# A layer's last modulation blocks, two weight splits and four row fetches moved to other places in the program

## The reference

```python
h = rms_norm(x, norm1) * (1 + sc1) + sh1
q, k, v, u = project(h, w_in)
x = x + g1 * (concat(attention(q, k, v), conv(u)) @ w_out)
h2 = rms_norm(x, norm2) * (1 + sc2) + sh2
x = x + g2 * peer(h2)          # 16384 single-neuron experts
# peer: per token 8 heads; each ranks 2 x 128 keys, takes the best 16 of the pair sums,
#       e = 16 expert numbers, g = softmax of their 16 scores; then
#       out = sum over the 128 slots of gelu(h2 . u_tab[e]) * g * v_tab[e]
```

## Time and profile before

| | us |
|---|---|
| median of 3 runs | 1755.14 (1753.58 to 1755.91) |
| the profiled execution | 1753.59 |
| its span, first to last instruction | 1751.8 |
| mean granted TensorE clock | 0.982 of full |

### The profile page before, as it was taken

How to read it: one execution, slowest core, us unless ns; L and a number is a source line. 1 busy time by engine, 2 the same in 40 slices (tenths; PEclk the granted TensorE clock), 3 DMA queues, 4 the chain that set the end, 5 groups by cost and what they waited for, 6 DMA issues and landing times.

```text
span 1751.8 us, 29907 instructions
## 1 busy us (share of the span) xinstructions
PE 1670.3 (95%) x9344; PEld 1407.0 (80%) x9344; DVE 1559.7 (89%) x3195; ACT 865.8 (49%) x2431; POOL 655.5 (37%) x644
## 2 busy tenths in 40 slices
PE   6999999999957889999999999999999999999997
PEld 4566777866636788888998989899999998999996
DVE  3887863499999989999999999999999999999998
ACT  3222574247787886444444444444444444444443
POOL 0000000034558874444444444444444444443442
PEclk9999999999977989999999999999999999999999
DMA  8343202111124878999999999999999999999996
GB/s 354 124 144 118 73 1 87 61 61 51 58 70 146 243 231 318 397 397 386 418 401 389 397 401 400 396 408 395 402 410 400 402 401 407 390 408 409 394 393 211
DMA packets 129316, 505.91 MB, mean 289 GB/s; under 512 B 9184, under 2 KB 64096, under 8 KB 79968
## 3 DMA queue, kind: packets, MB, share of 16 engines
q0 software_dynamic: 36864, 268.45, 38.0%
q1 hardware_dynamic: 92096, 236.49, 36.3%
q10 hardware_dynamic: 288, 0.13, 0.0%
HBM read 477.18 MB, written 25.10 MB: 287 GB/s over the span
## 4 chain that ended last, share of the span: by engine, by line
DVE 33%; DMA 22%; PE 21%; issue 19%; POOL 2%; ACT 1%; DVEq 1%; POOLq 0%; SPq 0%; ACTq 0%
DMA slab<-table,ixr 21%; DVE slab L1738 8%; PE psum L500 7%; DVE ulo L1629 4%; PE psum L735 3%; DVE slab L1688 3%; PE psum L823 3%; DVE slab L1728 3%; DVE vlo L1715 2%; DVE slab L1723 2%; PE psum L501 2%; PE psum L665 1%; DVE wlo L1711 1%; DVE slab L1543 1%; DVE slab L1692 1%
## 5 line engine op out<-in xcount | busy, mean ns | idle before, releaser
L1864 POOL DMA_INDIRECT slab<-table,ixr x256 | 421.5, 1647 | 608.0 <-DVE slab L1738 555.4
L844 PE MATMUL psum<-hhi,uhi 128*128 128x384 f32 x1008 | 339.2, 337 | 3.3 <-issue 3.2
L1728 DVE SCALAR_TENSOR_TENSOR slab<-slab,h2tok 128x1024 f32<-128x1024 f32 x256 | 312.3, 1220 | 29.3 <-DMA slab<-table,ixr 28.9
L844 PE MATMUL psum<-hhi,ulo 128*128 128x384 f32 x1008 | 338.1, 335 | 0.0
L844 PE MATMUL psum<-hlo,uhi 128*128 128x384 f32 x1008 | 337.6, 335 | 0.0
L1738 DVE SCALAR_TENSOR_TENSOR slab<-slab,cf 128x1024 f32<-128x1024 f32 x252 | 323.4, 1283 | 14.5
L858 PE MATMUL psum<-vhi,whi 128*128 128x512 f32 x762 | 297.2, 390 | 2.7 <-DVE wlo L1711 2.2
L858 PE MATMUL psum<-vhi,wlo 128*128 128x512 f32 x762 | 299.5, 393 | 0.0
L858 PE MATMUL psum<-vlo,whi 128*128 128x512 f32 x762 | 299.3, 393 | 0.0
L500 PE MATMUL psum<-slab 128*128 128x512 f32 x464 | 239.1, 597 | 2.1 <-ACT slab L925 1.7
L1203 ACT CAST whi<-slab 128x384 fp32r<-128x384 f32 x127 | 65.5, 515 | 305.6 <-DVE slab L1723 305.6
(11 more groups left out here) (237 smaller groups left out, 2824.2 us busy)
## 6 DMA issues: line engine op xcount, KB each, us to landing
slab<-ublk SPq DMA_DIRECT2D x64, 1024.0 KB, 9.3
slab<-vtab SPq DMA_DIRECT2D x63, 1024.0 KB
slab<-wblk SPq DMA_DIRECT2D x90, 512.0 KB, 4.6
g_dram<-slab SPq DMA_DIRECT2D x11, 1984.0 KB, 9.1
slab<-g_dram SPq DMA_DIRECT2D x31, 704.0 KB
slab<-table,ixr POOLq DMA_INDIRECT x256, 7.1
slab<-slab SPq DMA_DIRECT2D x42, 64.0 KB, 3.1
x<-x_in SPq DMA_DIRECT2D x1, 2560.0 KB, 9.7
```

Source lines behind the costliest of these rows:

```text
L844: last = pe.matmul(psum[:, b, 0:ND], w[:, c, :], m[:, c, :], start=(m_ == 0), stop=(m_ == 3 * DC - 1))
L1728: v.scalar_tensor_tensor(out=rows[:, sl % GR, 0:D], in0=rows[:, sl % GR, 0:D], scalar=1.0, in1=h2tok[:, k, :], op0=ALU.mult, op1=ALU.mult, ...
L1864: pool.indirect_dma_start(out=rows[:, sl % GR, :], out_offset=None, in_=table, in_offset=bass.IndirectOffsetOnAxis(ap=ixr[:, half, half_co ...
```

## The change

- TensorE: the last eight modulation blocks wait for `h2_tok` (the tokens copied out of banks 0 to 3) and no longer for `sk_read`; they use banks 0, 1 and 2 in place of 4, 5 and 6. The wait for `sk_read` now stands ahead of the turning of expert numbers, which uses banks 4 to 6 in place of 0 to 2.
- ScalarE: the first `u_lead` stands ahead of the last head's `weights_of`, the second right behind it, and both `copy_rows` behind that.
- GpSimd: the two first u rests are made inside the last `look_up`, ahead of its wait for `found`.
- The four row fetches of the build stand in blocks 2, 3, 4, 5, and `late_sums` and `row_numbers` behind blocks 0 and 1.
- The rest of u of step 2 is made by VectorE, at the head of `first_block`; GpSimd makes that of step 3 alone. In `first_block` the two dot products stand later.

```diff
-FETCH_AT = tuple(range(20, 20 + 16 * GR, 16))
+FETCH_AT = (2, 3, 4, 5)
...
-            pe.wait_ge(sk_read, SB)
+            pe.wait_ge(h2_tok, 2 * N_GATHER)
             for g in range(N_ADA3 // ADA_G):
-                ada(S_ADA3 + ADA_G * g, 4 + g)
+                ada(S_ADA3 + ADA_G * g, g)
             pe.wait_ge(row_copied, GROUPS1 + (N_ADA2 + N_ADA3) // ADA_G)
             for g in range(N_ADA3 // ADA_G):
-                last = ada_turn(modrow[2][:, g], 6, g)
+                last = ada_turn(modrow[2][:, g], 2, g)
             last.then_inc(ada_tp, 1)
-            pe.wait_ge(h2_tok, 2 * N_GATHER)
+            pe.wait_ge(sk_read, SB)
...
-            copy_rows(S_ADA3 + ADA_G, modrow[2][:, 0], 4)
-            weights_of(PH - 1)
-            copy_rows(S_ADA3 + 2 * ADA_G, modrow[2][:, 1], 5)
...
+            act.wait_ge(hsplit, 2)
+            u_lead(0, 0, True)
+            weights_of(PH - 1)
+            u_lead(1, 1, True)
+            for g in range(2):
+                copy_rows(S_ADA3 + ADA_G * (g + 1), modrow[2][:, g], g)
             act.activation(warm[:], ones[:, 0:1], ACT.Gelu)
...
-                    if k == 0 and within == 8:
+                    if k == 0 and within == 0:
                         late_sums()
-                    elif k == 0 and within == 12:
+                    elif k == 0 and within == 1:
                         row_numbers()
...
             def first_block():
...
+                v.wait_ge(ulo_set, 2)
+                u_rest(2, 2)
                 v.wait_ge(gel_set, 1)
...
                 v.tensor_tensor(wb[:, per:], wb[:, per:], gin[:, 0, per:, 0:TG], ALU.mult).then_inc(w_first, 1)
-                dot(0, 0, 0, 0)
...
-                dot(0, 0, 0, 1)
+                dot(0, 0, 0, 0)
                 v.wait_ge(whi_set, 1)
                 v.wait_ge(w_set, 1)
                 v.tensor_tensor(wlo[:, 0, 0:P], wgt[:, 0, 0:P], whi[:, 0, 0:P].bitcast(F32), ALU.subtract).then_inc(wlo_set, 1)
+                dot(0, 0, 0, 1)
...
                 pool.wait_ge(number_step, (i + 1) * NUMBER_STEPS)
+                if first is not None:
+                    first()
                 pool.wait_ge(found, 2 * i + 2)
...
+            def early_rests():
+                for n in range(2):
+                    pool.wait_ge(uhi_set, n + 1)
+                    pool.tensor_tensor(ulo[:, n], uraw[:, 0, n], uhi[:, n].bitcast(F32), ALU.subtract).then_inc(ulo_set, 1)
+
+            look_up(PH - 1, range(N_GATHER), last_early, last_late, half_last_early, half_last_late, early_rests)
...
-            for n in range(2, 4):
-                pool.wait_ge(uhi_set, n + 1)
-                pool.tensor_tensor(ulo[:, n], uraw[:, 1, n - 2], uhi[:, n - 2].bitcast(F32), ALU.subtract).then_inc(ulo_set, 1)
+            pool.wait_ge(uhi_set, 4)
+            pool.wait_ge(ulo_set, 3)
+            pool.tensor_tensor(ulo[:, 3], uraw[:, 1, 1], uhi[:, 1].bitcast(F32), ALU.subtract).then_inc(ulo_set, 1)
```

More of the change, by code:

```diff
@@ L810, in _ @@
                 pe.wait_ge(slot_summed, 1 + N_SUMMED * (PH - 1))
-                pe.transpose(psum[:, k, 0:P], ef[:, N_GATHER + k, :], ident)
-                pe.transpose(psum[:, k, P:2 * P], gw[:, N_GATHER + k, :], ident).then_inc(by_slot, 1)
+                pe.transpose(psum[:, 4 + k, 0:P], ef[:, N_GATHER + k, :], ident)
+                pe.transpose(psum[:, 4 + k, P:2 * P], gw[:, N_GATHER + k, :], ident).then_inc(by_slot, 1)
             pe.wait_ge(mod_set, GROUPS1 + 1 + N_MID)
@@ L1127, in u_lead @@
                 act.copy(uhi[:, jj % 2], uraw[:, jj // 2 % 2, jj % 2]).then_inc(uhi_set, 1)
+            act.wait_ge(hsplit, 2)
[4 more added lines that the diff above has]
+                copy_rows(S_ADA3 + ADA_G * (g + 1), modrow[2][:, g], g)
             act.activation(warm[:], ones[:, 0:1], ACT.Gelu)
-            act.wait_ge(hsplit, 2)
-            for n in range(2):
-                u_lead(n, n, True)
             for k in range(N_DENSE):
@@ L1135, in _ @@
                 act.wait_ge(by_slot, k + 1)
-                act.copy(eT[:, t * P:(t + 1) * P], psum[:, k, 0:P]).then_inc(slot_number, 1)
-                act.copy(gT[:, t * P:(t + 1) * P], psum[:, k, P:2 * P])
-                act.activation(gnT[:, t * P:(t + 1) * P], psum[:, k, P:2 * P], ACT.Copy, scale=-1.0).then_inc(slot_set, 1)
+                act.copy(eT[:, t * P:(t + 1) * P], psum[:, 4 + k, 0:P]).then_inc(slot_number, 1)
+                act.copy(gT[:, t * P:(t + 1) * P], psum[:, 4 + k, P:2 * P])
+                act.activation(gnT[:, t * P:(t + 1) * P], psum[:, 4 + k, P:2 * P], ACT.Copy, scale=-1.0).then_inc(slot_set, 1)
             def distance(b):
@@ L1645, in _ @@
             tried_numbers(2)
-            read_mod(2 + N_MID, 6, N_ADA3, M_G2)
+            read_mod(2 + N_MID, 2, N_ADA3, M_G2)
             dense_numbers(2)
@@ L1819, in _, with look_up @@
             pool.memset(ones[:], 1.0).then_inc(ones_set, 1)
-            def look_up(i, order, hit_early, hit_late, half_early, half_late):
+            def look_up(i, order, hit_early, hit_late, half_early, half_late, first=None):
                 pool.wait_ge(ranked, i + 1)
@@ L1855, in _ @@
                 look_up(i, (*range(N_GATHER, TILES), *range(N_GATHER)), hit_early, hit_late, half_early, half_late)
-            look_up(PH - 1, range(N_GATHER), last_early, last_late, half_last_early, half_last_late)
-            for n in range(2):
-                pool.wait_ge(uhi_set, n + 1)
-                pool.tensor_tensor(ulo[:, n], uraw[:, 0, n], uhi[:, n].bitcast(F32), ALU.subtract).then_inc(ulo_set, 1)
+            def early_rests():
[3 more added lines that the diff above has]
+            look_up(PH - 1, range(N_GATHER), last_early, last_late, half_last_early, half_last_late, early_rests)
             idxf = idxu[:].rearrange("p t s -> p (t s)")
```

## The result

| | before | changed |
|---|---|---|
| median of 5 runs each, us | 1754.84 (1753.58 to 1755.91) | 1744.42 (1741.99 to 1746.98) |
| the profiled execution, us | 1753.59 | 1741.99 |
| its span, us | 1751.8 | 1740.2 |
| mean granted TensorE clock | 0.982 | 0.985 |

The ratio is 0.9937, with an interval of 0.9924 to 0.995: 10.4 us faster, about 0.6%. The sign was right.

What follows compares the result with a forecast made beforehand. VectorE was taken to bound the build, TensorE the steps. Terms +1.05 - 5.1 - 0.1 - 2.0 + 1.1 = -5.05 us took 1753.59 to 1748.5, plus 1.55 for the median: 1750.1 us; range 1745.0 to 1756.5.

Steps and rivals of the forecast that it cites:

- build's start against H: From the last head's first placement (line 1591): GpSimd's early rests hold VectorE, so the build begins 1.05 us later.
- VectorE's waits in the build: Build: fetches moved ahead of the groups' exits remove VectorE's waits, -5.1 us; bounds -5.1 and -1.5.
- other work of the build: Build's fetch blocks: VectorE still makes all four rows there, 0.1 us less in total.
- lock at the build's end: Build's last block: three line 1688 instructions no longer meet GpSimd's rest of step 2, -2.0 us.
- path to the outputs of step 1: Build's end to TensorE's outputs: step 2's rest on VectorE lengthens it from 12.0 to 13.1 us, +1.1.
- one of my two orders: Last look-up: VectorE's placement first or GpSimd's rest first; either way the reductions start 3.9 us later.
- The first rival: Last look-up: GpSimd's rests don't hold the placement, build starts 2.9 us earlier, whole 1746.1 us; chance 0.20.
- Modulation, ScalarE and u: Heads: last modulation blocks end 11.9 us earlier, u lands about 521.1 us, the turns stay where they are.
- The fourth rival: Heads: u lands late, near 526 us, ScalarE holds the exponentials 2.3 us, whole 1752.4 us; chance 0.08.
- The first group: Build: first group leaves about 555.3 us, lands some 2 us late; ScalarE waits once, VectorE doesn't notice.
- The slower rival: Build: packed fetches block the first group, ScalarE stalls 11.5 us, whole 1759.9 us; chance 0.10.
- the transfers bind anyway: Build: groups out nearly fill the queue, so the 5.1 us come back elsewhere, whole 1755.2 us; chance 0.20.

Runs made afterwards that it cites:

- experiment 1: Kernel before with only the four row fetches moved to blocks 2 to 5, their numbers behind blocks 0 and 1: 1745.9 against 1752.81 us, ratio 0.9957.
- experiment 5: Kernel before with the four row fetches packed in blocks 44 to 47, mid-build: 1753.57 against 1754.62 us, ratio 0.9992.
- experiment 3: Kernel before with only the moved modulation, u splits during the last head and their rests inside the last look-up: 1755.09 us, ratio 1.0012.
- experiment 4: Changed kernel with the rests of steps 0 and 1 on VectorE behind its last placement: 1744.49 us, ratio 0.9948 to the kernel before.
- experiment 2: Kernel before with only step 2's rest on VectorE and the new `first_block`: 1752.61 us, ratio 0.9997.
- experiment 8: Changed kernel run again unchanged, against the kernel before: 1744.51 against 1754.62 us, ratio 0.9942.
- experiment 11: Changed kernel with all four early rests on VectorE, order otherwise kept: 1741.78 us against 1753.35 for the kernel before, ratio 0.9939.

## Why the prediction was wrong, point by point

| term, us | forecast | measured |
|---|---|---|
| build's start against H | +1.05 | +0.55 |
| VectorE's waits in the build | -5.1 | -7.7 |
| other work of the build | -0.1 | -1.7 |
| lock at the build's end | -2.0 | -2.1 |
| path to the outputs of step 1 | +1.1 | +0.98 |
| sum | -5.05 | -10.0 |

Measured is the mean of three profiles of the changed kernel less that of three of the kernel before: H to build 15.45 less 14.90, build 120.63 less 132.15, path 12.97 less 11.99. The waits are 0 against the mean of 5.1, 8.0 and 10.0; the lock is the 2.98 us of the earlier trace rows less the 0.84 that the same three instructions take now; the work left in the build is the 11.5 us less these 7.7 and 2.1. The 10.0 us compare with 10.4, 10.1 and 8.3 us in the medians of three sets of runs. The steps behind took 1066.9 to 1071.4 us in the changed kernel and 1069.5 to 1071.8 before; that spread between executions is larger than any difference between the two there, and within it what came earlier at step 1 came earlier at the end.

**The fetches: the step that failed.** The mechanism was right. Experiments 1 and 5 show it: moved ahead of the first group out, the fetches cause no wait of VectorE; packed in the middle they stop ScalarE once for 10.7 us. What failed is the size of the term -5.1 us: it is the waits of the one profiled execution, the shortest of three, and their mean is 7.7. That is 2.6 of the 5 us that the sum missed. The bounds failed with it: "-5.1 and ... -1.5" let the price go down only. The rows that I had would have set the other end. Four fetches of 2.9 us are 11.6 us of transfers, and each can delay an exit in full; the 5.1 us meant that slack swallowed more than half, and nothing said that it does so every time. With 11.6 in place of 5.1 as the far end the range would have begun at 1743.6.

**The other work of the build** was costed at 0.1 us and shrank by about 1.7, the second term that was mis-sized. Even against the first profile it is 1.5 us (129.37 less 120.65 is 8.7; less 5.1 and 2.1). Line 1688 fell from 92.8 to 89.5 us over 288 instructions, of which 2.1 is the lock at the end. Two kernels that keep this lock tell more. Without VectorE's waits, the builds with spread fetches last 124.3 to 124.6 us (profiles of the kernel before and experiment 3), experiment 1 lasts 122.8 and experiment 5 123.2; line 1688 takes 91.9 and 91.8 us in these two. So most of it comes with fetches in neighbouring blocks, early or not, and not with their place ahead of the exits. Why those instructions are shorter wasn't tested.

**The lock at the build's start: right in mechanism, 0.5 us off in size.** The cast and the second placement were held for 2.2 and 1.4 us. I had thought of the placement alone; the first got in before the rest began, as one of my two orders had it. The first rival (placement not held, build from about 537) is refuted by the build's start at 539.64 and by experiment 4. The page "SBUF — State Buffer" of the Trainium skill (section "SBUF: two separate sides") calls the shared port an exclusive lock that holds also operations with two SBUF inputs; the trace agrees, with 2.62 us against 1.20. Its page "Advanced Engine Details and Errata" (section "VectorE Performance Modes") names only the two-port modes as those that collide; lines 1591 and 1617, both of two inputs, were held, so here what that section lists is not complete.

**Modulation, ScalarE and u.** Blocks from 504.85 (505.4 forecast), u asked for at 515.76 (516.3); the first split is done by 524.2 and the copies by 527.8. As forecast, none of it moves the path: the turns start at 527.83 and wait 12.13 us for ScalarE's copies. The fourth rival (u late) didn't come about.

**The first group.** It left at 555.03 (555.3 forecast), with the fetches issued from 544.28 to 549.5. ScalarE didn't even have the one 2 us wait that I expected. The slower rival (an 11.5 us stall) falls, and so does "the transfers bind anyway": a group out took 8.9 us (median), and every exit kept up with the build.

**The end of the build.** The lock's 2.1 us went (2.98 less 0.87 is 2.1, where the prediction wrote 2.0), the path grew by 0.98 (1.1 forecast), TensorE's wait to 3.13 (3.5). What I had not seen is experiment 2: this edit by itself brings nothing that the times can tell.

## What to carry to other kernels

A wait that comes from transfers colliding is a sample from one execution: bound it above by all the transfers that can collide, not by the waits that one profile happens to show, and take a second profile of the same program where the term decides the sum. Put gathers of a known size where no later work waits for another transfer yet. Packing them among such transfers removed no wait here (9.4 us of waits, against 5.1 to 10.0 when spread); standing ahead of them removed all. A rest that GpSimd makes beside a busy VectorE isn't free: here VectorE loses less when it makes it itself.

## What the runs showed of the hardware

- Four 1 MB gathers among the 1984 KB stores cost an amount that differs between executions of the same program: the build took 129.37, 132.52 and 134.57 us. With the gathers ahead of the stores it took 120.61 to 120.65 us in three executions. Why the same order collides more in some executions stays open.
- The lock catches small work too, with one input as well as two. A cast of 128x40 waited 2.2 us for one 128x1024 subtraction of GpSimd. Two such subtractions cost VectorE 3.0 us in lines 1653 and 1654, 3.6 in 1600 and 1591, and 3.65 in 1617; VectorE makes one in 1.14 us to the next start (line 1629 at 660.29), GpSimd in some 2.4.
- TensorE's granted clock was 1.00 from 600 us to the end of a build without stalls. Behind the wait ahead of step 1 it was not the same in every execution of the changed kernel: over the first 7.8 us of outputs it was 0.62 and 0.61 behind waits of 3.13 us, and 1.00 behind one of 3.10 us in experiment 8. So the wait alone doesn't tell whether the clock falls; in experiment 11 it was 1.00 behind 1.03 us. The first outputs of experiment 8 take 0.47 us where the changed kernel's first profile has 0.77:

```profile
672.50 0.47 PE L858 MATMUL psum<-vhi,whi 128*128 128x512 f32 x1 [3.10 <-DVE wlo L1711]
```
